# A mixture-of-experts kernel: the first expert's weights loaded a stage earlier, rows gathered by products of a reordered x

## What is computed

```
g_w, g_idx = top_k(softmax(x @ w_rg + b_rg), 1)              # 4 groups
e_w, e_idx = top_k(softmax(expert logits of that group), 2)  # 8 experts a group
x_rows     = x[row_tok]                                      # blocks of rows of one expert
y_rows     = (silu(xb @ w_gate[e]) * (xb @ w_up[e])) @ w_down[e]
y          = segment_sum(y_rows * row_gate)
```

## Time and profile before

| | |
|---|---|
| median of 3 runs | 4311.12 us (4306.35 to 4319.81) |
| profiled execution | 4322.71 us, span 4321.0 us |
| busy, of the span | PE 94%, PE weight loads 63%, DVE 42%, ACT 16%, POOL 18% |
| mean granted TensorE clock | 0.969 |
| memory traffic | HBM read 643.71 MB, written 27.54 MB |
| three loads an expert | x65 each, 2048.0 KB, median 17.9 to 21.2 us from issue to landing |

### The profile page before, as it was taken

The page is one execution under the profiler, slowest core; times in us unless marked ns, Lnnn a source line. Parts: engine busy times, 40 slices in busy tenths (PEclk is TensorE's granted clock), DMA queues, the critical chain, the costliest instruction groups (busy, mean ns, idle before and its releaser), DMA issues. The chain is left out here.

```text
span 4321.0 us, 62282 instructions
## 1 busy us (share of the span) xinstructions
PE 4043.9 (94%) x26498; PEld 2718.4 (63%) x26498; DVE 1799.4 (42%) x3229; ACT 698.6 (16%) x1496; POOL 792.1 (18%) x647
## 2 busy tenths in 40 slices
PE   6999999999999888999999999899996999799995
PEld 4478885786445786886445884455445987444442
DVE  6667756551248465321244061412215335522223
ACT  2202111100023122110021150100002013200001
POOL 1123213432010120542010020000003334200001
PEclk8999989999999999999999999999997999899998
DMA  4221212652112001222112202699992210399996
GB/s 139 68 77 63 84 46 102 218 182 103 58 59 68 31 2 54 88 88 102 59 61 72 67 1 88 273 421 421 421 407 92 89 50 1 152 411 421 421 421 269
DMA packets 238512, 675.27 MB, mean 156 GB/s; under 512 B 19897, under 2 KB 134145, under 8 KB 188317
## 3 DMA queue, kind: packets, MB, share of 16 engines
q1 hardware_dynamic: 222138, 635.17, 38.3%
q10 hardware_dynamic: 13796, 27.74, 1.7%
q0 software_dynamic: 2304, 8.39, 0.5%
HBM read 643.71 MB, written 27.54 MB: 155 GB/s over the span
## 5 line engine op out<-in xcount | busy, mean ns | idle before, releaser
L3296 PE MATMUL experts_pg<-moe_wg,experts_xt 128*64 128x256 f32 x4160 | 463.2, 380 | 3.8 <-DVE experts_xt L3412 2.2
L3296 PEld LDWEIGHTS experts_pg<-moe_wg,experts_xt 128*64 128x64 f32 x4160 | 298.6, 137 | 184.0 <-issue 37.5
L645 PE MATMUL ffn_out_y<-ffn_out_ring,ffn_h 128*128 128x512 f32 x640 | 275.9, 593 | 0.0
L3276 PE MATMUL experts_pxg<-x_tok,experts_sel 128*64 128x512 f32 x1072 | 260.8, 609 | 3.1 <-DVE experts_sel L3479 3.1
L3313 PE MATMUL experts_py<-moe_wd,experts_ht 128*64 128x512 f32 x1040 | 248.6, 599 | 0.0
L746 PE MATMUL ffn_in_seven<-ffn_in_seven_t,ffn_in_seven_s 128*128 128x256 f32 x1056 | 237.6, 381 | 1.7 <-DVE ffn_in_seven_t L819 0.8
L746 PEld LDWEIGHTS ffn_in_seven<-ffn_in_seven_t,ffn_in_seven_s 128*128 128x128 f32 x1056 | 201.3, 191 | 31.5 <-DVE ffn_in_seven_t L819 1.6
L3418 DVE TENSOR_TENSOR experts_h<-experts_hs,experts_pg 128x256 f32<-128x256 f32 x65 | 27.4, 421 | 460.6 <-PE experts_pg L3296 460.5
L645 PEld LDWEIGHTS ffn_out_y<-ffn_out_ring,ffn_h 128*128 128x128 f32 x640 | 121.2, 190 | 151.4 <-issue 150.1
L3552 POOL DMA_INDIRECT merge_yg<-y_rows,moe_yi x16 | 16.4, 1026 | 1056.7 <-PEq L3537 534.8
L746 PE MATMUL ffn_in_seven<-ut,ffn_in_ring 128*128 128x256 f32 x672 | 164.8, 389 | 0.0
(11 more groups left out here) (762 smaller groups left out, 7102.0 us busy)
## 6 DMA issues: line engine op xcount, KB each, us to landing
moe_wg<-in_moe_w_gate SPq DMA_DIRECT2D x65, 2048.0 KB, 19.7
moe_wg<-in_moe_w_up SPq DMA_DIRECT2D x65, 2048.0 KB, 21.2
moe_wd<-in_moe_w_down SPq DMA_DIRECT2D x65, 2048.0 KB, 17.9
ffn_in_ring<-in_ffn_w_in SPq DMA_DIRECT2D x42, 1024.0 KB, 5.0
ffn_in_ada_ring<-in_ada_w SPq DMA_DIRECT2D x28, 1024.0 KB, 6.8
ffn_out_ring<-in_ffn_w_out SPq DMA_DIRECT2D x20, 1024.0 KB, 4.9
ssd_proj_ring<-in_ssd_w_in SPq DMA_DIRECT2D x19, 1024.0 KB, 5.1
att_kqt<-in_attn_w_qkv SPq DMA_DIRECT2D x17, 1024.0 KB, 4.8
```

The costliest lines, as they stand in the source:

```text
L645: last = nc.tensor.matmul(y[:, tt, half, :], h[:, kk, tt * P:(tt + 1) * P], ring[n][:, q, half * BANK:(half + 1) * BANK], start=(kk == 0), ...
L3276: last = nc.tensor.matmul(pxg[half * SLOTS:(half + 1) * SLOTS, :], sel[:, q, tt, b * SLOTS:(b + 1) * SLOTS], k.x[:, tt, half * HALF:(half ...
L3296: last = nc.tensor.matmul(pg[ch * SLOTS:(ch + 1) * SLOTS, b, side, 0:HH], xt[:, b, kk, :], gate_up(w, side)[:, kk, ch * HH:(ch + 1) * HH], ...
```

## The change

`First` is a new tile of one expert's weights that lives from the SSD stages to the end. Its space holds `feat` in SSD and `kqt` in attention. It becomes weight slot 0 of both MoE layers, and slot 1 is a tile of the same size. Expert 0 is loaded into it on SP in the norm stage ahead of each MoE layer, and at the start of `experts` SP issues expert 1 alone. ACT copies x into `by_row` (the space of `k.ut`) with each half's features in another order. The rows of a pair of experts are gathered at once and come out turned: the stationary operand is 128 tokens by 128 features of `by_row`, the moving one `sel` of 128 seats. The turning of rows and one of two DVE copies a block go away. Half a pair's products are made in each block.

```diff
@@ project_norm_stage
+                if router is not None:
+                    k.first.load(sp, router)
                 norm.store(sp)
@@ ssd_stages, attention_stages
-            feat, xdt, bt = mix.sb("feat", [P, N_FEAT, T]), mix.sb("xdt", [P, TT, SSD_INNER]), mix.sb("bt", [P, TT, G * N])
+            feat = k.first.tile[:, :].rearrange("p (m t) -> p m t", m=N_FEAT)
+            xdt, bt = mix.sb("xdt", [P, TT, SSD_INNER]), mix.sb("bt", [P, TT, G * N])
-        kqt = outer.sb("kqt", [P, G, 2, 4, R, P])
+        kqt = k.first.tile[:, :].rearrange("p (g a m r n) -> p g a m r n", g=G, a=2, m=4, r=R)
@@ moe_stages, SP
-                    for n in range(2):
-                        w, _ = slot(n)
-                        load_gate(sp, one_of(n), w)
-                        load_up(sp, one_of(n), w)
-                        load_down(sp, one_of(n), w)
+                    load_gate(sp, one_of(1), 1)
+                    load_up(sp, one_of(1), 1)
+                    load_down(sp, one_of(1), 1)
@@ moe_stages, PE
-                    def gather(n, selected, b, q, part, first=False):
...
-                        for tt in range(part * TT // 2, (part + 1) * TT // 2):
-                            for half in range(2):
-                                last = nc.tensor.matmul(pxg[half * SLOTS:(half + 1) * SLOTS, :], sel[:, q, tt, b * SLOTS:(b + 1) * SLOTS],
-                                                        k.x[:, tt, half * HALF:(half + 1) * HALF], start=(tt == 0), stop=(tt == TT - 1))
...
-                    def turn_rows(n, first=False):
...
+                    def units(half, m, selected, q, width, taken):
...
+                        for kk in range(half * QUARTER + m, half * QUARTER + m + 2):
+                            for tt in range(TT):
+                                last = nc.tensor.matmul(px[:, kk, 0:width], by_row[:, tt, half, kk % QUARTER, :], sel[:, q, tt, 0:width],
+                                                        start=(tt == 0), stop=(tt == TT - 1))
+                        if m == 2:
+                            last.then_inc(s["xt_made"], 1)
...
+                    pe.wait_ge(s["sorted"], TT)
+                    for half in range(2):
+                        for m_ in (0, 2):
+                            units(half, m_, 1, 0, P, None)
...
+                    def pair_ahead(p, half):
+                        width = P if p < PAIRS else SLOTS
+                        return lambda part: units(half, 2 * part, p + 1, p % 2, width, 2 * p + half - 1)
@@ moe_stages, ACT
+                    act.wait_ge(s["logits_made"], 1)
+                    for tt in range(TT):
+                        act.activation(by_row[:, tt, :, :, :], k.x[:, tt, :].rearrange("p (h n m) -> p h m n", h=2, m=QUARTER), ACT.Copy).then_inc(s["sorted"], 1)
@@ moe_stages, DVE
-                    def take_rows(n, first=False):
...
-                    def take_turned(n, b):
...
+                    def take(half, q, width, made):
+                        dve.wait_ge(s["xt_made"], made)
+                        V.tensor_copy(xt[:, q, half * QUARTER:(half + 1) * QUARTER, 0:width],
+                                      px[:, half * QUARTER:(half + 1) * QUARTER, 0:width]).then_inc(s["xt_taken"], 1)
@@ new
+    def load(self, sp, l):
+        for n in range(3):
+            sp.dma_start(self.halves(self.part(self.tile, n)), self.source(l, n)[:, 0, :, :]).then_inc(self.sems[n], 16)
```

More of the change, by code:

```diff
@@ L3177, in gate_up @@
         def gate_up(w, side):
-            return wg[:, w, side, :, :]
+            return First.part(k.first.tile if w == 0 else second, side)
         def down(w):
-            return wd[:, w, :, :]
-        halves = lambda w: w.rearrange("p (h k) n -> p h (k n)", h=2)
+            return First.part(k.first.tile if w == 0 else second, 2)
+        halves = First.halves
         def load_gate(sp, e, w):
@@ L3281, in turn_rows @@
-                    def turn_rows(n, first=False):
[L3282 to L3287, removed]
-                    def one(n, b, w, use, ahead=None, first=False):
-                        pe.wait_ge(s["xt_taken"], n + 1)
+                        if taken is not None:
+                            pe.wait_ge(s["xt_taken"], taken)
@@ new lines, in units, with one @@
+                        for kk in range(half * QUARTER + m, half * QUARTER + m + 2):
[4 more added lines that the diff above has]
+                            last.then_inc(s["xt_made"], 1)
+                    def one(n, b, w, use, q, seat_at, taken, ahead, first=False):
+                        pe.wait_ge(s["xt_taken"], taken)
@@ L3304, in one @@
                         last.then_inc(s["ht_made"], 1)
-                        if ahead is not None:
-                            gather(n + 1, *ahead, 1)
+                        ahead(1)
                         pe.wait_ge(s["ht_taken"], n + 1)
-                        pe.wait_ge(down_in[w], 16 * use + 16)
-                        if not first:
+                        if first:
+                            k.first.wait(pe, 2, l)
+                        else:
+                            pe.wait_ge(down_in[w], 16 * use + 16 * w)
                             pe.wait_ge(s["y_taken"], n)
@@ L3513, in _ @@
                         one(n, n % 2, n // 2)
-                        take_rows(n + 1)
-                        take_turned(n + 1, (n + 1) % 2)
+                        p, half = n // 2 + 1, n % 2
+                        if p <= PAIRS:
+                            take(half, p % 2, P if p < PAIRS else SLOTS, 2 * p + half + 1)
+                        else:
+                            for half in range(2):
+                                take(half, 1, SLOTS, 2 * n - (2 * PAIRS - 3) + half)
                         if n % 2 == 0 and n // 2 + 2 < PAIRS:
@@ L3522, in _ @@
                         one(it, 1, it - (WRITTEN - ODD))
-                        take_rows(it + 1)
-                        take_turned(it + 1, 1)
+                        for half in range(2):
+                            take(half, 1, SLOTS, 2 * it - (2 * PAIRS - 3) + half)
                         select_block(it + 2, 1)
@@ L3658, in program @@
         ffn_stages(nc, k, 1, a["ffn_w_in"][1], a["ffn_w_out"][1], ga_dram[1, 1], a["ln_g"][1, 1], a["ln_b"][1, 1], *after(3), ada([]))
+        k.first = First(sb("first_expert", [P, First.SIZE]), [kept.sem(f"first_{n}_in") for n in ("gate", "up", "down")], a)
         ssd_stages(nc, k, a, a["ln_g_2"][0, 0], a["ln_b_2"][0, 0], *after(4))
@@ L3662, in program, with __init__, part, halves @@
         moe_stages(nc, k, a, 1, *after(7))
+class First:
+    SIZE = 3 * D * MOE_HIDDEN // P
+    def __init__(self, tile, sems, a):
+        self.tile, self.sems, self.a = tile, sems, a
+    @staticmethod
+    def part(tile, n):
+        size = First.SIZE // 3
+        return tile[:, n * size:(n + 1) * size].rearrange("p (k n) -> p k n", k=(DK, DK, MOE_HIDDEN // P)[n])
+    @staticmethod
+    def halves(w):
+        return w.rearrange("p (h k) n -> p h (k n)", h=2)
+    def source(self, l, part):
+        name = ("moe_w_gate_2", "moe_w_up_2", "moe_w_down_2")[part]
+        return self.a[name][l].rearrange("e (h p k) n -> p e h (k n)", p=P, h=2)
+    def load(self, sp, l):
+        for n in range(3):
+            sp.dma_start(self.halves(self.part(self.tile, n)), self.source(l, n)[:, 0, :, :]).then_inc(self.sems[n], 16)
+    def wait(self, eng, part, l):
+        eng.wait_ge(self.sems[part], 16 * (l + 1))
 class Router:
```

60 lines of the change are left out of this document (25 added, 35 removed).

## The result

| | before | after |
|---|---|---|
| median, runs of the same chip | 4312.38 us (4306.35 to 4322.06) | 4317.07 us (4310.36 to 4324.98) |
| profiled execution | 4322.71 us, span 4321.0 us | 4315.81 us, span 4314.1 us |
| bytes moved in full slices | 421 GB/s | 425 GB/s |

The ratio is 1.0013, interval 1.0007 to 1.0019: **5.6 us slower** (3.0 to 8.2), where the forecast was no change (+0.2 us). It lies inside the range and inside the 0.3% that was called "same", and yet the interval leaves no doubt that something costs. A second measurement of the same kernel gave 1.0008 (0.9997 to 1.0019).

The account below looks back on a forecast made before the run. The weight stream at 421 GB/s, 15.6 us a block, was taken to bound the MoE layers. Layer 0's +1.0 and layer 1's -0.8 us sum to +0.2, called none: 4311 us, range 4298 to 4325 for 8 in 10.

Parts of the forecast that it names:

- In come 16 products, which are 32 instructions ... 3.69 us: PE's work per MoE block: new gather products take 3.69 us, replacing 4.27 us of gathering and turning; period 15.19 to 14.6 us.
- in each of 63 blocks: PE's 0.6 us saving a block, 37 us in all, costed at nothing because the weight stream's 15.6 us covers it.
- except for the last block of each layer ... -0.6 us a layer: End of each MoE layer: the last block runs behind its last weights, so PE's saving counts there, -0.6 us a layer.
- 421 GB/s as before: Sign expected in the changed profile: the weight stream in the MoE layers keeps its rate of 421 GB/s.
- The first rival: MoE layers: the stream runs faster than PE, so PE's saving shows, 37 us less in steady blocks, 4276 us; chance 0.09.
- Layer 1's -2.5 us: Start of MoE layer 1: credit for 2.5 us of stream lost in the kernel before, with its slow block 0.
- The bound in the changed kernel: MoE layers: stream sets the pace; from about block 16 PE waits for gate weights, some 15 us a layer.
- The preload's account: Start of MoE layers: 14.9 us of loads leave each, but the stream stands still 15.4 us in layer 0, 16.0 in layer 1.
- The gather of 64 instructions: First gather of each MoE layer: clock rises partway; 4.3 plus 5.1 us in layer 0, 5.8 plus 4.3 us in layer 1.
- the slow rival: First gather of each MoE layer stays at half clock, 14.0 us; +8.1 and +7.4 us, total 4326.5 us; chance 0.10.
- The price of the products: PE's gather products: 0.115 us an instruction by attention's row, against about 81 ns by the skill's page.
- ACT's passes: ACT's reordering before the first gather: four passes of 1.24 us, 5.0 us under the routing; if doubled, +1 us a layer.

Follow-up runs that it names:

- old_tail: Changed kernel, but blocks whose rows are gathered singly get them gathered and turned as before; ratio 0.9988 to the kernel before, median 4307.0 us.
- half_tail: Changed kernel, single blocks' rows summed over two of four token tiles, 16 products instead of 32; ratio 0.9987 to the kernel before, median 4305.9 us.
- load_at_start: Changed kernel, but expert 0 is loaded at the start of the MoE stage as before; ratio 1.0020 to the kernel before, median 4322.1 us.
- slots_first: Kernel before with its two weight tiles allocated ahead of the MoE stage's small tiles; ratio 0.9985 (0.9974 to 0.9996) to the kernel before.
- before_again: The kernel before run and profiled once more, no edit; ratio 1.0001 (0.9989 to 1.0013).
- third_gate_ahead: Changed kernel with old single-block gather, a third gate-weight place, and each next expert's gate load issued ahead of up and down loads; ratio 0.9979 to the kernel before.
- after_again: The changed kernel run and profiled once more, no edit; ratio 1.0008 (0.9997 to 1.0019) to the kernel before.
- third_gate: Changed kernel with the old single-block gather and a third place for gate weights, load order kept; ratio 0.9985 to the kernel before, median 4307.4 us.

## Why the prediction was wrong by 5 us

**The step that failed: "In come 16 products, which are 32 instructions ... 3.69 us", "in each of 63 blocks", and from it "except for the last block of each layer ... -0.6 us a layer".** It holds for a block whose successor is in a pair: the period there is 14.49 us (forecast 14.6). Half a pair's products, 32 instructions, are made in each of two blocks. But a single block has no partner to share them with, and `block_ahead` makes both halves in one block: 32 products, 64 instructions. The `for m_ in (0, 2)` inside `part(half)` of the kernel (shown under `old_tail`) says so, and I had read over it; the description above, "half a pair's products are made in each block", has the same gap. This happens from block 30 on: in block 30 for block 31, in layer 1 also in block 31 for block 32, and in each layer's last block for one that doesn't exist, since the loop gathers ahead without knowing its end. That makes two such blocks in layer 0 and three in layer 1. In each of them the products take 3.63 + 3.61 us where the forecast had 3.69 us in all, and the tails of the layers came out 1.5 and 2.5 us longer than before, not 0.6 shorter. The products have 64 columns instead of 128 there, which saves next to nothing (0.113 us for 0.117 an instruction); both load 128 columns of weights.

Such a block needs 18.0 us on PE, more than the stream's 15.4. The last one of a layer is paid as a longer tail, the others (one and two) as a longer period. Against the forecast, in us:

| | layer 0 | layer 1 |
|---|---|---|
| forecast | +1.0 | -0.8 |
| tail: 14.6 measured; forecast 13.1 - 0.6 and 12.1 - 0.6 | +2.1 | +3.1 |
| other such blocks: 18.9 (layer 0), 18.2 and 18.0 (layer 1) for 15.6 each | +3.3 | +5.0 |
| stream at 425 for 421 GB/s: 15.42 for 15.57 us, some 30 blocks | -4.5 | -4.5 |
| block 28's up products at the fallen clock, net | | +0.6 |
| sum | +1.9 | +3.4 |
| measured against the first profile (514.0 - 512.6; 532.6 - 529.9) | +1.4 | +2.7 |

The terms account for the sign and most of the size; 0.5 and 0.7 us of them are not found in the layers' ends and aren't assigned. The stream's -4.5 us is worked out from the two rates and no run shows it by itself. Taken away as a whole, the single blocks' products gave 4.6 and 7.5 us (`old_tail`), 5.3 and 8.9 us (`half_tail`).

**"421 GB/s as before"** was wrong in the other direction. The first rival was near that: the stream did give way, but by 0.9% and not below PE's period, and not because of fewer loads: `load_at_start`, with as many loads as before, has 425 as well, and `slots_first` gets its 426 by the place of the tiles alone. By the table the rate hid 9.0 of the 13.5 us that the single blocks cost. Of the figures of the Trainium skill, page "DMA: Bandwidth & Descriptors", section "Specifications", the 435 GB/s of the fabric stand above both measured rates and the 358 GB/s for HBM to one core under both.

**Layer 1's -2.5 us** for a slow start of before holds for some executions only. In `before_again` the clock rose during the gather and stayed, and the third gate load came at 27.5 us, not 30.7. Against that execution the change loses 6.3 us in layer 1 and 2.3 in layer 0, sum 8.6; against the first one 2.7 and 1.4, sum 4.1. The ratio's 5.6 us lies between, as it would if the clock does the one in some executions and the other in others.

**What held.** The bound in the changed kernel: the stream, with PE waiting from block 15 on (forecast 16), 11 to 12 us a layer (forecast 15), though for up weights and not for gate weights. In the kernel before the two limits lie closer than the forecast put them: `before_again` waited 0.5 us for weights in the last block of each layer and hardly at all before. The preload's account: third gate load at +30.1 us (forecast +30.3), a stream that stood still from 2742 to 2756, and under 1 us a layer for the whole preload, by undoing it. The gather of 64 instructions: 9.33 us in layer 0 and 9.81 us in layer 1 (forecast 9.4 and 10.1), never the 14 us of the slow rival. The price of the products: forecast 0.115 us by attention's row; the steady group of 16 instructions took 1.88 us from start to next start (2773.33 to 2775.21), or 0.117 each. The trace does not agree with the 81 ns that the Trainium skill gives in "TensorE: Matmul & The Clock Gate", section "Back-to-back issue gap". ACT's passes at 1.94 us each, nearer the doubled 2.5 than the 1.24, ended under the routing. The norm stages were no longer with the moved loads than without.

## What to carry to other kernels

When a loop's work is written as "half a pair per step", count the steps that have no pair, and look for them at the end: behind a stream the last blocks are the only ones whose PE time is paid, and 3.6 us more in two or three of 32 blocks cost 12 us over two layers, while 0.7 us less in each of the others was worth 1.6 and 1.4 us a layer. A preload is worth the idle time of the stream that it removes, not its bytes: here the freed 14.9 us became a hole, because the next load waits for PE, and only more places together with another order of the queue (`third_gate_ahead`) took a little of it. And before crediting a change with a gain or a loss in a stream, try the kernel before with its tiles in the other order: that alone measured 0.15% here, beside the 0.13% that the whole change lost.

## What the runs showed of the hardware that was not expected

- **The place of the destination in SBUF changes the rate of a stream.** With the slots behind the stage's small tiles (680 bytes a partition) it is 421 GB/s in all four kernels profiled so, with them at the front 426 (`slots_first`), and with one of two slots ahead of those tiles 425, in all nine such executions. From 2850 to 3150 us the median of the 8 KB packets is 312 ns in `before` and 309 in `slots_first`, and the slow ones (319 ns at the 90th percentile) vanish. 24 bytes higher didn't do it. Which boundary it is that counts wasn't found.
- **A product of 64 columns takes nearly as long as one of 128** where both load 128 columns of weights: 0.113 us an instruction beside 0.117.
- **The granted clock can fall behind a short burst or not in the same code:** block 0's gate and up products took 8.79 us in one execution (granted clock 0.50 from 3771 to 3773 us), 7.13 in the other, behind a gather of 6.52 and of 4.97 us. With the longer gather of the change the third gate load came at 30.1 to 30.6 us in all four layers profiled.
- **A wait of about 2 us for weights can cost the clock, and need not.** Behind waits of 2.00 us (`after`), 1.92 (`after_again`) and 2.26 (`third_gate`, layer 1) 32 instructions took 5.36 us; behind the 2.45 us in `third_gate_ahead` they took 3.67. Waits of 0.5 to 0.8 us cost none, nor did one of 1.46 us in `old_tail`. What decides isn't shown.
- **A copy on ACT that reads every fourth element** took 1.94 us for 128x1024, where another operation of ACT on as many elements, in order, took 1.24 us.
